# The compression nets' first layer in four 32-column groups of the array

## What is computed

```python
def compress(x, pe, w1, w2):           # CMP_BLOCK 32, CMP_STRIDE 16, hd 128, CMP_HIDDEN 256
    ...
    blocks = blocks + pe[None, None, :, None, :].astype(x.dtype)
    flat = blocks.transpose(0, 1, 3, 2, 4).reshape(B, n_cmp, G, CMP_BLOCK * hd)
    return jax.nn.silu(flat @ w1) @ w2
```

## Time and profile before

| | us |
|---|---|
| median of three runs | 1261.48 (1261.21 to 1264.48) |
| profiled execution, its time | 1261.58 |
| its span in the trace | 1260.3 |
| TensorE busy | 1168.4 (93%) |
| weight loads busy | 1042.9 (83%) |
| VectorE busy | 751.7 (60%) |
| ScalarE busy | 599.8 (48%) |
| matmuls of L744 busy | 28.7 |

### The profile page before, as it was taken

How to read it: one execution, slowest core, us unless ns; L and a number is a source line. 1 busy time by engine, 2 the same in 40 slices (tenths; PEclk the granted TensorE clock), 3 DMA queues, 4 the chain that set the end, 5 groups by cost and what they waited for, 6 DMA issues and landing times.

```text
span 1260.3 us, 19031 instructions
## 1 busy us (share of the span) xinstructions
PE 1168.4 (93%) x7674; PEld 1042.9 (83%) x7674; DVE 751.7 (60%) x1416; ACT 599.8 (48%) x1059; POOL 31.1 (2%) x30
## 2 busy tenths in 40 slices
PE   6899989899988999998988899999979979999998
PEld 3777789888878999887977789998868957999976
DVE  3643467687767788665455666665444445566653
ACT  2332358445546565544434465444454345645443
POOL 0320100000000000001000000000000000000000
PEclk9799999899988999998979899999979979999999
DMA  8736343444324555555432155554534303655450
GB/s 340 295 139 251 142 183 143 149 173 171 134 100 149 171 194 173 186 201 214 168 118 101 68 217 203 180 189 157 194 119 154 130 3 132 217 171 197 151 184 34
DMA packets 30507, 207.78 MB, mean 165 GB/s; under 512 B 3507, under 2 KB 4019, under 8 KB 6612
## 3 DMA queue, kind: packets, MB, share of 16 engines
q1 hardware_dynamic: 30420, 206.56, 45.2%
HBM read 205.50 MB, written 1.05 MB: 164 GB/s over the span
## 4 chain that ended last, share of the span: by engine, by line
PE 80%; DVE 11%; ACT 5%; issue 3%; DMA 1%; SPq 0%; POOL 0%; ACTq 0%; DVEq 0%
PE ps L391 47%; PE ps L1507 17%; DVE wlo L350 2%; PE ps L409 2%; PE ps L744 2%; ACT whi L343 1%; DVE tm L549 1%; PE ps L2116 1%; PE ps L2084 1%; PE ps L510 1%; ACT sq L1522 1%; PE ps L1630 1%; PE ps L1213 1%; DMA raw<-ada 1%; PE ps L1922 1%
## 5 line engine op out<-in xcount | busy, mean ns | idle before, releaser
L350 DVE TENSOR_TENSOR wlo<-raw,whi 128x1024 fp32r<-128x1024 f32 x324 | 371.1, 1188 | 250.7 <-ACT whi L343 250.6
L391 PE MATMUL ps<-H_h,whi 128*128 128x256 f32 x1648 | 478.4, 290 | 5.3 <-DVE H_l L494 4.3
L391 PE MATMUL ps<-H_l,whi 128*128 128x256 f32 x1648 | 471.5, 286 | 0.0
L391 PE MATMUL ps<-H_h,wlo 128*128 128x256 f32 x1648 | 471.3, 286 | 0.0
L343 ACT ACTIVATE whi<-raw 128x1024 fp32r<-128x1024 f32 x324 | 314.6, 1020 | 167.0 <-PE ps L1507 121.7
L391 PEld LDWEIGHTS ps<-H_h,whi 128*128 128x128 f32 x1648 | 322.1, 195 | 9.4 <-issue 7.8
L391 PEld LDWEIGHTS ps<-H_l,whi 128*128 128x128 f32 x1648 | 321.9, 195 | 0.5 <-issue 0.2
L391 PEld LDWEIGHTS ps<-H_h,wlo 128*128 128x128 f32 x1648 | 321.6, 195 | 0.0
L1507 PE MATMUL ps<-whi,gl_h 128*128 128x512 f32 x264 | 106.2, 402 | 2.8 <-DVE wlo L350 2.8
L1507 PE MATMUL ps<-wlo,gl_h 128*128 128x512 f32 x264 | 105.1, 398 | 0.0
L1507 PE MATMUL ps<-whi,gl_l 128*128 128x512 f32 x264 | 104.9, 397 | 0.0
(11 more groups left out here) (411 smaller groups left out, 1444.4 us busy)
## 6 DMA issues: line engine op xcount, KB each, us to landing
raw<-f SPq DMA_DIRECT2D x44, 1024.0 KB, 4.9
raw<-win SPq DMA_DIRECT2D x33, 1024.0 KB, 5.5
raw<-ada SPq DMA_DIRECT2D x24, 1024.0 KB, 5.5
raw<-up SPq DMA_DIRECT2D x22, 1024.0 KB, 4.8
raw<-g SPq DMA_DIRECT2D x20, 1024.0 KB, 4.8
raw<-pw SPq DMA_DIRECT2D x12, 1024.0 KB, 4.8
raw<-down SPq DMA_DIRECT2D x10, 1024.0 KB, 4.9
raw<-ck SPq DMA_DIRECT2D x4, 1024.0 KB, 7.1
```

What stands on the lines that cost most here:

```text
L350: dve.tensor_tensor(wlo[j % NS][:, a:b], raw_of(key)[:, a:b], whi[j % NS][:, a:b].bitcast(F32), ALU.subtract).then_inc(w_lo.hit(key, half), 1)
L391: ins_ = pe.matmul(bank[:, m * 256:(m + 1) * 256], wt[a][:, kt * w + col + m * 128:kt * w + col + m * 128 + 128], act[b][:, k0 + kt, :], s ...
```

## The change

Position jj goes to column group jj % 4 of the array, and its product to the 32 partitions of bank 7 that belong to that group. So each group holds the sum over eight of the 32 positions, in the same eight matmuls a unit as before. The four partial sums are copied in one instruction of 128 partitions (L752), and the two transposes become two ordinary fp32 products with a constant `fold`, four identities of 32 one below the other, which transposes and adds the four in one. `xb` is padded from 30 to 32 blocks, the two added ones are set to zero on GpSimd, and TensorE waits for that once for each net.

```diff
-    hrow = [sb(f"hrow{i}", [30, 256]) for i in range(2)]
-    xb = [sb(f"xb{i}", [128, 32, 30]) for i in range(2)]
+    hrow = [sb(f"hrow{i}", [128, 256]) for i in range(2)]
+    xb = [sb(f"xb{i}", [128, 32, 32]) for i in range(2)]
...
             pe.wait_ge(*xb_set(kv))
+            pe.wait_ge(*zeroed("xb", kv))
...
-            ins_ = pe.matmul(banks[7][0:30, 0:256], xb[kv][:, jj, :], raw_of(key)[:, j * 256:j * 256 + 256], start=jj == 0,
-                             stop=jj == 31)
+            g = 32 * (jj % 4)
+            ins_ = pe.matmul(banks[7][g:g + 32, 0:256], xb[kv][:, jj, :], raw_of(key)[:, j * 256:j * 256 + 256],
+                             start=jj < 4, stop=jj >= 28, tile_position=(0, g))
...
-        act.activation(hrow[kv][:], banks[7][0:30, 0:256], ACT.Copy).then_inc(cmp_row.hit(kv), 1)
+        act.activation(hrow[kv][:], banks[7][:, 0:256], ACT.Copy).then_inc(cmp_row.hit(kv), 1)
...
-        pe.transpose(b[:, 0:30], hrow[kv][:, 0:128], cc("ident")[0:30, 0:30])
-        pe.transpose(b[:, 32:62], hrow[kv][:, 128:256], cc("ident")[0:30, 0:30]).then_inc(cmp_turn.hit(kv), 1)
+        pe.matmul(b[:, 0:32], hrow[kv][:, 0:128], cc("fold"), start=True, stop=True)
+        pe.matmul(b[:, 32:64], hrow[kv][:, 128:256], cc("fold"), start=True, stop=True).then_inc(cmp_turn.hit(kv), 1)
...
         pool.memset(mkr[:], 0.0).then_inc(zeroed.hit("mkr"), 1)
+        for kv in range(2):
+            pool.memset(xb[kv][:, :, 30:32], 0.0).then_inc(zeroed.hit("xb", kv), 1)
...
+    put("fold", np.tile(np.eye(32), (4, 1)))
```

More of the change, by code:

```diff
@@ L36 @@
                ("cos", 256), ("sin", 256), ("cosr", 256), ("sinr", 256), ("mask2", 256), ("tri", 256),
-               ("cadd", 30), ("cmul", 30)]:
+               ("cadd", 30), ("cmul", 30), ("fold", 32)]:
     CT_[_n] = (NCON, _k)
```

## The result

The changed kernel takes 1242.35 us (median of four runs, 1241.41 to 1243.45), the kernel before 1262.36 us (1261.21 to 1264.48). The ratio is 0.984, with a 95% interval of 0.982 to 0.985. It is 20.0 us faster, where 10.5 were forecast; the time lies under the range's low end of 1246, and within 1 us of that of the rival in which all four groups work at once (1241.4).

What follows compares the result with a forecast made beforehand. TensorE's 28.36 us in L744 were taken to be on the path; runs of 17.8 us gain 10.6, the fold adds 0.13: -10.5 us from 1261.58 gives 1251.1 us, range 1246 to 1262.5.

Steps and rivals of the forecast that it cites:

- the rival in which all four groups work at once: L744's runs: four products cost two passes, 0.432 us; runs 8.0 us, gain 20.4, total 1241.4 us; chance 0.08.
- the overlap: L744's 64 products: starts in program order, two groups busy at a time, 0.216 + 0.031 us a product, 15.8 us.
- the uncovered pass at the end of each run: L744's six runs: each ends with a pass nobody overlaps, 6 x 0.216 = 1.3 us.
- the ends of the bound: A neighbour's start in L744 costs 0.004 us if weights load early, or one weight load, 0.031 us (taken).
- Never sooner: Weight loads on TensorE: a load starts as the matmul before it starts, never sooner, so a neighbour costs 0.031 us.
- the draining rival: L744's 64 borders between products: each group change drains, nothing overlaps, slower, 1263.7 to 1274.1 us; chance 0.10.
- no overlap: L744: fp32 matmuls of two groups don't share the array; runs stay 28.4 us, total 1261.7 us; chance 0.17.
- The fold: L760 and L761 become four passes, about 0.36 us: +0.13 us for the first net, second covered by ScalarE.
- Padding, waits, windows, constants: GpSimd memsets, TensorE's added waits, window writes at 128 bytes' distance and 32 more constant columns: each taken as 0.
- What is late next: TensorE's feeders: 1.4 us left for the square of `key_act`, 1.8 for the last head's square; neither late.
- The clock: Granted clock, 1.00 in this stretch, dips to 0.7 later may shift: taken as 0, 2 us each way in the range.
- theory D: From the experiments, not the prediction: passes enter their group's queue of four in program order; a full queue stops everything behind.

Runs made afterwards that it cites:

- pairs: The changed kernel with two neighbouring positions sharing one of the four groups (jj // 2 % 4): 1242.02 us, ratio 0.9834 to the kernel before.
- fours: The changed kernel with four neighbouring positions sharing one of the four groups (jj // 4 % 4): 1253.29 us, ratio 0.9916 to the kernel before.
- eights: The changed kernel with each unit of eight positions in one group (jj // 8): 1262.00 us, ratio 0.9991 to the kernel before.
- threes: The changed kernel with two groups a unit, in the order 0 0 0 1 1 1 0 1: 1251.67 us, ratio 0.9906 to the kernel before.
- the last experiment: The changed kernel plus four column groups for L510's products in the first four conditioning-weight units: 1236.74 us, ratio 0.9795 to the kernel before.

## Why the prediction was wrong

**The bound was right.** TensorE's 28.36 us in L744 were on the path, and what was taken from them came off the time: 20.43 us in the trace, 20.0 in the medians of before and after, and the kernel with one group is back at the time of before. The direction was right too.

**The step that failed is the overlap**, at the sentence "I assume that matmuls start in the order of the program, as all rows do". From it followed that a product's second pass, waiting for its first, keeps the neighbour's first pass waiting too, so that two groups work at a time and a product costs 0.216 + 0.031 us. The runs show that a pass waits only for its own group. A product costs 2 x 0.216 / 4 = 0.108 us, and 64 of them 6.9 us instead of the 15.8 of the sum; the uncovered pass at the end of each run, another 1.3, doesn't exist either. These two terms are 10.2 us too much; the runs' ends took 0.2 more than the 0.7 of the sum, and 17.8 - 7.79 = 10.0 is the miss in the runs. In the time it shows as 8.75 us, 1251.1 against 1242.35. The rows that I took as evidence couldn't bear it: all have one group only, and in one group there is nothing to overtake. So the ends of the bound (0.004 and 0.031 us a neighbour) were both ends of one mechanism, and the other mechanism had got a chance of 0.08. The Trainium skill (TensorE: Matmul & The Clock Gate, What overlaps and what doesn't) also has matmuls in the program's order in start and end; the runs with pairs, fours, eights and threes disagree.

**Loads.** "Never sooner" than the matmul before starts is true in one group. In four, eight loads begin beside the first four matmuls. The rule of the Trainium skill (TensorE: Matmul & The Clock Gate, What overlaps and what doesn't) by which the draining rival would have held, that loads overlap only where the row group differs, isn't met in the changed kernel either: its four groups use all rows. The rival is out, and so is no overlap.

**The rival of four at once** had 6.9 + 0.7 + 0.4 = 8.0 us for the runs, and 7.79 was measured. It was priced rightly and ranked wrongly. The Trainium skill (TensorEngine Tiling (Array Packing), Theoretical Speedup) with its up to 4x agrees: 4 x 0.215 us is what 16 passes cost, and fp32's two passes don't take from it.

**The fold**: 0.36 us as predicted, +0.13 on the path for the first net, none for the second. **Padding, waits, windows, constants**: priced at nothing. The run with one group bears it out, 1.0004. In the changed kernel the windows take 8.32 us against 8.30, and GpSimd still idles 4.17 us ahead of them. `con` had 2236 columns (the 1118 KB of the earlier trace rows), not 2364, which changes nothing. **The copy** of 128 partitions takes 0.385 us against 0.372, off the path. The piece ahead of the first run is 0.52 us in both.

**What is late next**: nothing on the path, as predicted, but with less in hand than I had reckoned. The runs got shorter than forecast, and the unit that was issued at 99.18 was landed and its split begun 5.32 us later, instead of 4.87. ScalarE's split of this unit is the closest call. In the changed kernel:

```profile
104.50 2.01 ACT L343 ACTIVATE whi<-raw 128x1024 fp32r<-128x1024 f32 x2 [4.27 <-DMA raw<-win]
106.41 0.18 ACT L797 ACTIVATE sq<-ps 128x30 f32<-128x30 f32 x1
...
109.38 0.58 ACT L678 ACTIVATE zt<-ps 128x512 f32<-128x512 f32 x1
109.86 0.59 ACT L684 ACTIVATE sq<-ps 128x512 f32<-128x512 f32 x1
```

The split is done at 106.51, and TensorE had finished L789 at 106.28, so the square comes about 0.1 us later than it could; its reader is only needed at 109.95. I had forecast 1.4 us in hand there. For the last head's square I had 1.8; it ends at 110.45, 0.5 us after the last run's end at 109.95. That costs nothing either: L700 begins only at 111.06. What L693 reads, `zt`, is ready at 109.96, 0.13 us before L693's load begins at 110.09.

**The clock** was priced at 0 with 2 us each way. In this pair of traces it gave most of 3.6 us in the head and took 2.7 behind. The first unit of L510 is the same code in all kernels but the last experiment, and takes between 4.96 and 6.50 us in their traces. The eight passes of L823 or L825 take 1.03 us in the traces of before, one group, two groups and the last experiment, 1.31 in that of the eights, and 1.86 in those of the changed kernel, the pairs, the fours and the threes. With one trace of each kernel I can't say whether the second place follows from the edits or varies by itself. What the executions show is that a kernel's time moves with its mean clock: the kernel with eights takes 1257.9 to 1258.8 us at 0.958 and 1263.2 to 1264.9 at 0.953, the kernel before some 1261.1 to 1262.8 at 0.956 and 1262.9 to 1264.8 at 0.954. All four executions of the changed kernel were at 0.954. So a difference of two medians can hold some 2 us of clock, and that 20.0 comes so near to 20.43 is partly luck.

## What to carry to other kernels

A matmul with at most 32 stationary columns uses a quarter of the array's columns for its whole time. A sum over many of them can be dealt out to four column groups, with one small product to add the four. Here that brought fp32 products of 256 moving columns from 28.36 to 7.79 us, near a quarter; other types and lengths weren't run. It comes off the kernel's time where TensorE is on the path, as it was here. Deal the products in turn, or at most four passes in a row for one group. And where a trace shows only one instance of a resource, it says nothing about order between two: price the mechanisms apart, not just two ends of one.

## What the runs showed of the hardware

The rows don't name the group of a matmul, so this rests on the timings and on the passes of 403 ns. Each run but the first has as many of these as it has groups: one in the kernel before and with one group, four in the changed kernel, and two or four in the runs with two groups, fours, eights and threes, but for the single units of the eights, which have one group and one such pass. Matmuls of different column groups overtake each other: a group's first pass started beside another's that stood twelve passes ahead of it in the program, 0.04 us after the run's first (pairs). Each group has room for four passes (or two products of two passes) with the running one. Behind six, eight and sixteen passes of one group, another group's first came two, four and twelve pass lengths late (runs of 2.31, 2.74 and 6.19 us). Four fp32 matmuls that read four different blocks of moving data at once are not slower than one, 0.216 us a pass in both.

From this I infer that the last matmul of a program need not be the last to finish, if its group had less to do. By theory D it was the last in all kernels run here, and what a semaphore on it would say otherwise wasn't tried.
